# Score products of a chunked recurrence alternate between the two row halves of TensorE

## The reference, cut to what matters

```python
def step(state, inp):
    r_t, w_t, k_t, v_t, a_t, b_t = inp
    sa = jnp.einsum('bhvk,bhk->bhv', state, a_t)
    state = (state * w_t[:, :, None, :]
             + sa[..., None] * b_t[:, :, None, :]
             + v_t[..., None] * k_t[:, :, None, :])
    y_t = jnp.einsum('bhvk,bhk->bhv', state, r_t)
    return state, y_t
```

## Time and profile before

| | |
|---|---|
| median of 3 runs | 2552.99 us |
| lowest and highest | 2545.66 and 2556.85 us |
| span of the profiled execution | 2554.0 us |
| PE busy | 2325.7 us (91% of the span) |
| DVE, ACT, POOL busy | 969.0, 794.8, 790.0 us |
| mean granted TensorE clock | 0.929 |

### The profile page before, as it was taken

The page is one execution under the profiler, slowest core; times in us unless marked ns, Lnnn a source line. Parts: engine busy times, 40 slices in busy tenths (PEclk is TensorE's granted clock), DMA queues, the critical chain, the costliest instruction groups (busy, mean ns, idle before and its releaser), DMA issues.

```text
span 2554.0 us, 29794 instructions
## 1 busy us (share of the span) xinstructions
PE 2325.7 (91%) x12156; PEld 1828.0 (72%) x12156; DVE 969.0 (38%) x1432; ACT 794.8 (31%) x1079; POOL 790.0 (31%) x287
## 2 busy tenths in 40 slices
PE   5997589999979999999889878999999899888987
PEld 3885089999945788888656644788888787667765
DVE  5237954444434322210235674322210233422433
ACT  4335411211222344421322253433421333213232
POOL 2330442332510344343332101244444241222420
PEclk8998599999985999999999887999999899798999
DMA  3220000000010233323221100333332221122210
GB/s 120 81 69 11 4 1 1 1 1 2 1 60 16 75 91 99 99 91 105 76 66 66 34 1 17 83 99 90 91 105 93 83 83 50 33 87 66 67 50 33
DMA packets 190680, 146.83 MB, mean 57 GB/s; under 512 B 6888, under 2 KB 188351, under 8 KB 190576
## 3 DMA queue, kind: packets, MB, share of 16 engines
q1 hardware_dynamic: 190576, 145.34, 18.5%
HBM read 143.22 MB, written 2.10 MB: 57 GB/s over the span
## 4 chain that ended last, share of the span: by engine, by line
PE 78%; DVE 13%; ACT 4%; POOL 2%; issue 2%; DMA 1%; SPq 0%; DVEq 0%; ACTq 0%
PE psum L2082 18%; PE psum L2083 17%; PE psum L2084 17%; DVE X_lo L1503 3%; PE psum L2282 3%; PE psum L2267 3%; PE psum L2277 2%; PE psum L2240 1%; POOL w_lo L935 1%; DVE xf L1628 1%; PE psum L2158 1%; ACT w_hi L1066 1%; PE psum L2327 1%; PE psum L2321 1%; PE psum L2435 1%
## 5 line engine op out<-in xcount | busy, mean ns | idle before, releaser
L935 POOL TENSOR_TENSOR w_lo<-weight_raw,w_hi 128x2048 fp32r<-128x2048 f32 (+3 forms) x136 | 605.1, 4450 | 1384.4 <-ACT w_hi L1066 1384.2
L2082 PE MATMUL psum<-X_hi,w_hi 128*128 128x512 f32 x1544 | 641.4, 415 | 67.8 <-DVE X_lo L1503 43.9
L2083 PE MATMUL psum<-X_lo,w_hi 128*128 128x512 f32 x1544 | 616.6, 399 | 0.0
L2084 PE MATMUL psum<-X_hi,w_lo 128*128 128x512 f32 x1544 | 615.4, 399 | 0.0
L2082 PEld LDWEIGHTS psum<-X_hi,w_hi 128*128 128x128 f32 x1544 | 298.9, 194 | 176.1 <-issue 89.0
L1066 ACT ACTIVATE w_hi<-weight_raw 128x2048 fp32r<-128x2048 f32 (+3 forms) x136 | 251.9, 1852 | 361.3 <-PE psum L2084 349.7
L2083 PEld LDWEIGHTS psum<-X_lo,w_hi 128*128 128x128 f32 x1544 | 299.6, 194 | 65.0 <-issue 6.7
L2084 PEld LDWEIGHTS psum<-X_hi,w_lo 128*128 128x128 f32 x1544 | 298.9, 194 | 65.3
L1552 DVE TENSOR_TENSOR sgate<-rt,psum 128x512 f32<-128x512 f32 x44 | 30.2, 687 | 320.5 <-PE psum L2084 320.5
L2082 PE MATMUL psum<-hb_hi,w_hi 128*128 128x512 f32 x352 | 136.9, 389 | 0.0
L2083 PE MATMUL psum<-hb_lo,w_hi 128*128 128x512 f32 x352 | 136.9, 389 | 0.0
(11 more groups left out here) (424 smaller groups left out, 3372.0 us busy)
## 6 DMA issues: line engine op xcount, KB each, us to landing
weight_raw<-in_ffn_w_gu SPq DMA_DIRECT2D x88, 512.0 KB, 4.5
weight_raw<-in_l_w_in SPq DMA_DIRECT2D x45, 512.0 KB, 4.6
weight_raw<-in_ffn_w_down SPq DMA_DIRECT2D x40, 512.0 KB, 3.6
weight_raw<-in_kv_w SPq DMA_DIRECT2D x16, 512.0 KB, 3.9
weight_raw<-in_l_w_out SPq DMA_DIRECT2D x16, 512.0 KB, 4.0
weight_raw<-in_rw_w_k SPq DMA_DIRECT2D x8, 512.0 KB, 6.8
weight_raw<-in_rw_w_v SPq DMA_DIRECT2D x8, 512.0 KB, 4.4
weight_raw<-in_rw_w_r SPq DMA_DIRECT2D x8, 512.0 KB, 4.3
```

The lines of the kernel that those rows point to most:

```text
L935: ins = pool.tensor_tensor(l, r, h.bitcast(F32), ALU.subtract)
L2082: pe.matmul(ps, wh, xh, start=start, stop=False, skip_group_check=True)
L2083: pe.matmul(ps, wh, xl, start=False, stop=False, skip_group_check=True)
L2084: return pe.matmul(ps, wl, xh, start=False, stop=stop, skip_group_check=True)
```

## The change

The score stage is written in another order. Before, all four kinds of the first group came before the four kinds of the second. Now a kind is formed for both groups before the next kind, and its eight matmuls alternate between the two groups, and so between the two row halves and between two banks. The list of jobs and DVE's masks follow the same order. Nothing is added or taken away: there are as many matmuls, loads, masks and waits as before. The lines after the edit have moved by one to two (L2240 is L2241 in the changed kernel, L1704 is L1705).

```diff
@@ make_jobs
-            for g in gs:
-                for m in ("At", "Rb", "Ak", "Rk"):
+            for m in ("At", "Rb", "Ak", "Rk"):
+                for g in gs:
                     core((m, tt, g), "D")
@@ vector
-                    for g in gs:
-                        for m, dst, mask in (("At", At[:, g % 2, :], strict), ("Rb", Rb[:, g, :], incl),
-                                             ("Ak", Ak[:, g % 2, :], strict), ("Rk", Rk[:, g, :], incl)):
+                    for m, dst_of, mask in (("At", lambda g: At[:, g % 2, :], strict), ("Rb", lambda g: Rb[:, g, :], incl),
+                                            ("Ak", lambda g: Ak[:, g % 2, :], strict), ("Rk", lambda g: Rk[:, g, :], incl)):
+                        for g in gs:
+                            dst = dst_of(g)
                             key = (m, tt, g)
@@ tensor
-                    for g in gs:
-                        for m, left, right in (("At", af, u0), ("Rb", af, rf), ("Ak", kf, u0), ("Rk", kf, rf)):
-                            b = begin((m, tt, g))
-                            for j in range(4):
+                    for m, left, right in (("At", af, u0), ("Rb", af, rf), ("Ak", kf, u0), ("Rk", kf, rf)):
+                        banks = [begin((m, tt, g)) for g in gs]
+                        for j in range(4):
+                            for b, g in zip(banks, gs):
                                 hd = group_head(g, j)
                                 rows = slice(64 * (hd % 2), 64 * (hd % 2) + 64)
                                 ins = pe.matmul(psum[:, b, P * j:P * j + P], left[rows, hd // 2, tk],
                                                 right[rows, hd // 2, tk], start=True, stop=True,
                                                 skip_group_check=True)
-                            ins.then_inc(job_done, 1)
+                                if j == 3:
+                                    ins.then_inc(job_done, 1)
```

## The result

The changed kernel takes 2573.53 us (median of 4 runs, 2568.48 to 2577.05) against 2552.85 us; the ratio is 1.0074, with a 95% interval of 1.0049 to 1.0099. I had forecast 2556.6 us, within 2545 to 2566, so the direction of the sum was right and its size was not: +20.7 us instead of +3.6. It is the slower rival's figure, 2574.8 us, that came out.

What follows compares the result with a forecast made beforehand. PE was taken to bound the kernel (78% of the span). Clock falls of 9.0 us less a gain of 5.4 us gave +3.6 us on the median of 2552.99, so 2556.6 us, range 2545 to 2566.

Steps and rivals of the forecast that it cites:

- Matmuls, masks, POOL: Score stage: matmuls last 3.57 us, DVE's masks follow every 0.61 us, POOL's chain ends at 7.24 instead of 7.86.
- The gain of 5.4 us: Score stages: second T1 starts at 7.25 instead of 7.92; about 0.68 us kept a stage, 8 x 0.68, if clock stays.
- Rival 3: Score stage: halves don't overlap when alternating matmul by matmul; POOL's chain ends at 8.13, +2 us, 2555 us; chance 0.05.
- the emptying of PSUM as the bound: Score stage: by a Trainium skill rule, DVE's masks would bound, ending 1.65 us earlier; gain 8 x 1.65 = 13.2 us.
- Rival 1: Recurrence: the clock stays at 1.00 despite the gaps, so only the gain is left, 2547.6 us; chance 0.30.
- 6 x 1.5 = 9.0 us more: Behind score stages: two idle gaps make the clock fall to 0.50 in 6 stages of 8, costing 1.5 us each.
- Rival 2: Behind each score stage: clock falls and stays down, 6.8 us in all eight stages, +21.8, 2574.8 us; chance 0.10.

Runs made afterwards that it cites:

- AV first: Changed kernel with the two AV jobs put before the two transposes of Tt, in the job list, on PE and on ACT: 2544.51 us, ratio 0.9959.
- steps on DVE: Changed kernel with the inverse's first two steps (L982, L983) of each pair's second group done by DVE instead of POOL: 2558.56 us, ratio 1.0016.
- alternating by four: Changed kernel, but within a kind one group's four matmuls come before the other group's four: 2562.85 us, ratio 1.0022.
- AV of 128 columns: Changed kernel with all but one of AV's matmuls streaming 128 columns instead of 64: 2562.58 us, ratio 1.0025.
- POOL late: Kernel before the change with POOL's L982 done twice for each group, halves not alternating: 2591.28 us, ratio 1.014.

## Why the prediction was wrong

- **Matmuls, masks, POOL.** Right, each within 0.1 us: 3.57 us of scores, masks at 0.6 us, second transposes at 7.28 (7.21 in the other stages), gaps of 0.8 to 0.9 and 1.9 us. The gain of 5.4 us, forecast for a clock that stays, was measured as 5.6 where the gaps were filled.
- **Rival 3, no overlap, and the emptying of PSUM as the bound.** Both excluded: two groups of a kind took 1.06 us together, and the last mask ended at 6.1 us, more than a microsecond before the last transposes.
- **Rival 1, the clock stays.** Its mechanism exists, but with this order of the stage it needed the second gap closed at least by half (2547 to 2551 us, forecast 2547.6). The section "Why this matters for your kernels" of the Trainium skill's page "TensorE: Matmul & The Clock Gate" warns of longer single gaps. Read as in the prediction, as if shorter ones were safe, it isn't borne out by the trace: 0.80 to 0.87 and 1.91 us, with 0.66 us of work between them, were followed by a fall in eight stages of eight, and so was a single gap of 2.25 us.
- **The step that failed** is the term "6 x 1.5 = 9.0 us more". The mechanism was right and the size wrong: the falls cost 24.5 us, 2.7 times as much. There were 8 falls instead of 6, and they lasted 6.8 us on average instead of 3.4, so each cost 3.1 us instead of 1.5. The count was a guess below the rows, which had three falls of three. The length was carried over from the attention stage. There the work behind the gaps streams 128 columns and more, in the recurrence it is AV with 64, as the order of a tile in "The kernel before" says, and I didn't ask about it. And the term counted a fall that begins inside the wait as the cheaper one. It is the longer one, and the trace of the kernel before had a row for it in the same attention stage. Behind gaps of 1.02 and 1.55 us the fall began 1.0 us ahead of the second gap's end and lasted 6.8 us:

```profile
1470.06 0.46 PE L2435 MATMUL psum<-PTs,av 128*128 128x128 f32 x2 [1.02 <-ACT PTs L1365]
...
1472.71 1.19 PE L2435 MATMUL psum<-PTs,av 128*128 128x128 f32 x4 [1.55 <-ACT PTs L1365]
...
1471.70:1478.50 6.80, 5.79 (x23) 4.51 (x25) 4.62 (x15) 3.52 (x13) 0.00 (x0) 0.50 0.00 0
```

- **Rival 2** has the right price (8 x 3.4 - 5.4 = +21.8 us) and had 0.10. I let it decide by whether PE is free of gaps during the fall. It was free of them (6.80 of 6.80 us busy) and the clock stayed down all the same. The 58 us of the earlier trace rows at clock 0.50, with PE busy for 52.14 of them, were a hint that a busy PE isn't enough, though a weak one, since it had 5.9 us of idle time. So the rival's number came out within 1.3 us of the measured 2573.5, but not for its reason that further gaps would follow: part of that is luck.

## What to carry to other kernels

A shorter stage on TensorE is worth only what the next engine in the chain leaves of it, and the rest becomes idle time. If gaps of 1 to 2 us come into work that was dense, price the clock's fall in both number and length, by where it begins and by what PE does right behind the gap, before counting the gain. When the idle time is there, move real work that doesn't wait for the slow engine into it; a filler of useless matmuls is the quick test of whether the clock is the cause.

## What the runs showed of the hardware

- Matmuls in the two row halves, alternating one by one and into two banks, run fully at once: 16 records in 1.06 us where one half alone needs 1.05 for 8. Even with four by four, a few matmuls at each change of half overlap.
- The clock behind idle gaps of PE, by the profiled executions (eight stages each):

| gaps in a stage, us | stages with a fall | at 0.50 in all, us |
|---|---|---|
| 0.26 (kernel before) | 0 | 0 |
| 0.9 | 0 | 0 |
| 0.6, 0.4 and 0.6 (AV first) | 0 | 0 |
| 0.9 and 1.0 | 0 | 0 |
| 1.1 and 1.2 (steps on DVE) | 6 | 30.7 |
| 1.6 (alternating by four) | 6 | 37.6 |
| 1.9 | 4 | 20.5 |
| 0.8 and 1.9, AV of 128 columns | 6 | 23.9 |
| 0.8 and 1.9 (changed kernel) | 8 | 54.6 |
| 2.25 (POOL late) | 8 | 54.6 |

- The same gaps hit one stage and not the next, and 1.6 us hit more stages than 1.9. So no single length of a gap decides in these runs, and why a stage is spared stays open.
- A fall that began 0.1 to 1.0 us behind the end of the last gap lasted 6.8 us with matmuls of 64 columns there (eleven falls in four kernels) and 3.4 with the same number at 128 columns (three falls). One that began 0.7 us or more ahead of that end lasted 10.2 us with 64 columns (three falls) and 6.8 with 128 (one).
- DVE's operations on two SBUF tiles of 128x512 took 1.20 to 1.33 and 1.64 us while POOL worked, and POOL slowed from 1.27 to 1.59 us beside them. With POOL idle such an operation took 0.69 us (L1749 of the same run), as long as a mask out of PSUM.
